# Two transformer blocks on one core: how the split fp32r operands are laid out in on-chip memory

## The chip, the cores and the metric

The kernel runs on one core of one Trainium2 chip. The metric is the device time of one execution in microseconds. Before the change it is 1729.82 us (median of 3 runs, 1728.46 to 1733.68).

## What is computed

512 tokens of width 1024 pass through two different blocks. The first adds 16 meta tokens in front (528 positions), projects, runs sliding-window attention, forgetting attention and a gated linear recurrence, merges the three, and ends with a gated feed-forward layer. The second projects again, runs a chunked mLSTM and differential attention, merges them, and ends with 32 routed experts of which each token uses two.

```python
def reference(x, ...):
    x = first_block(x, ...)   # 512 tokens and 16 meta tokens
    return second_block(x, ...)

# first_block
u = rms_norm(h, norm_mix[l]);  proj = u @ w_in[l]
merged = (g[:, :, 0] * (o_a @ w_branch[l, 0]) + g[:, :, 1] * (o_f @ w_branch[l, 1])
          + g[:, :, 2] * (o_c @ w_branch[l, 2]))
h = h + merged @ w_out[l]
gate_ff, up_ff = jnp.split(rms_norm(h, norm_ffn[l]) @ w_ffn_in[l], 2, axis=-1)
h = h + (jax.nn.silu(gate_ff) * up_ff) @ w_ffn_out[l]

# second_block
proj = (rmsnorm(x, norm1_w[l]) * (1.0 + scale1) + shift1) @ w_in[l]
merged = jax.nn.sigmoid(g_m) * (hm @ w_br_m[l]) + jax.nn.sigmoid(g_d) * (hd @ w_br_d[l])
x = x + gate1 * (merged @ w_out[l])
x = x + gate2 * hierarchical_moe(h2, ...)
```

## The kernel before

**The dense products.** Every dense weight matrix comes in slabs of 1 MB: 8 chunks of 128 rows by 256 columns (4 by 512 for the branch products, 2 by 1024 for `w_ffn_out`). SyncE loads slab `h` into `raw`, ScalarE rounds it to fp32r in `WH` (L976), VectorE writes the rest into `WL` (L1506), which has the same place as `raw`. The activations are split in the same way into a high and a low part. A group of outputs (one PSUM bank, 128 features by 512 tokens) takes three matmuls for each chunk of the contraction, in `split3`: high weight by high activation (L2365), high weight by low activation (L2366), low weight by high activation (L2367). With 8 chunks a group has 24 matmuls. In the trace's names the moving operand stands first: `psum<-AH,WH` streams AH against weights WH. Only the value projections (`vf`, `vm`, `vd`) turn this round: the activations are loaded as weights and 256 columns of WH or WL are streamed.

**The order.** The list `SLABS` of `plan_dense` sets it: `xc`, `fl`, `kf` (positions in two halves of 264 columns), `vf`, `qf`, `yc`, `qa`, `kava`, the gates and branches of the first block, `wo`, the feed-forward pair `ffg`/`ffu`, `ffo`, then the second block's projections, gates, branches, `wo2`, and last the expert loop. TensorE runs the list in order. In the two mixing stretches (MIX_FLOW, FLOW2) one piece of a dense group (12 matmuls, or a whole group of a branch) is followed by a few attention matmuls, in an order that is written out by hand.

**Where the operands lie.** Tensors stand at fixed places, in KB from a common base (`at(name, kb, shape)`). The places of the operands of `split3` (a view of AHt from column 16 starts 64 B into the row):

| tensor | place, KB | row | used by |
|---|---|---|---|
| AH (view of AHt from column 16) | 26 | 528 columns, 2112 B | all projections, `wo`, `ffg`/`ffu`, second block, `wo2` |
| AL (same view of ALt) | 42.5 | 2112 B | the same |
| WL / raw, 3 buffers of 8 KB | 59 | 1 KB or 2 KB | all |
| WH, 2 buffers of 8 KB | 83 | the same | all |
| OH | 99 + 52.8125 + 42.75 = 194.5625 | 512 columns, 2048 B | first block's branches |
| OL0, OL1, OL2 | 99, 107, 115 | 2048 B | the same |
| FH, FLo | 99, 143 | 2048 B | `ffo` |
| AHu, ALu | 146.5, 162.5 | 2048 B | `ffg` 0 and `ffu` 0 only |
| OH2, OL2 | 107, 115 | 2048 B | second block's branches |

Of the kernel before, what the change touches and what calls it, by code (L numbers as in the profile page):

```python
# [16 lines left out]
F32 = mybir.dt.float32  # L17
F32R = mybir.dt.float32r
BF16 = mybir.dt.bfloat16
I32 = mybir.dt.int32  # L20
U32 = mybir.dt.uint32
ALU = mybir.AluOpType
# [3 lines left out]
P = 128  # L26
D = 1024
KC = D // P
S = 512
M = 16  # L30
T = S + M
# [3 lines left out]
C1 = W1 // P  # L35
# [197 lines left out]
SLAB_OF = {s["name"]: s for s in SLABS}  # L233
# [136 lines left out]
def build_program(nc, a, out):  # L370

    ctx = ExitStack()
    with ctx:
# [15 lines left out]
        def at(name, kb, shape, dt=F32):  # L389
            return nc.alloc_sbuf_tensor_at(name, [P] + list(shape), dt, offset=int(base + kb * KB))[:]  # L390


        cst = at("cst", 0, [CTOT])
        pcol = at("pcol", 5.5, [2 * P])
        ones = at("ones", 6.5, [P])
        small = at("small", 7.0, [256])
        identb = at("identb", 8.0, [P], BF16)
        maskb = at("maskb", 8.25, [P], BF16)
        maskT = at("maskT", 9.5, [P])
        sinkb = at("sinkb", 8.5, [16])  # L400
        rel = at("rel", 8.5625, [8])
        fbias = at("fbias", 8.625, [4])
        mod = at("mod", 8.75, [48])
        rb = at("rb", 9.0, [36])
        stat = at("stat", 9.25, [64])
        hT = at("hT", 10, [KC, S])

        AHt = at("AH", 26, [KC, T], F32R)
        ALt = at("AL", 42.5, [KC, T], F32R)
        AH, AL = AHt[:, :, M:], ALt[:, :, M:]  # L410
        raw = at("raw", 59, [RAW, SLAB])

        WL = at("WL", 59, [RAW, SLAB], F32R)
# [16 lines left out]
        Z0 = W0 + 52.8125  # L430
        stage = at("stage", W0, [8, SKEW])
        utmp = at("utmp", Z0 + 12, [2, S])
# [6 lines left out]
        Sb = at("Sb", Z0 + 16.5, [4, 400])  # L439
        PT = at("PT", Z0 + 22.75, [2, 4 * P])  # L440
        merged = at("merged", Z0 + 26.75, [KC, S])
        OH = at("OH", Z0 + 42.75, [C1, S], F32R)
        g1a = at("g1a", Z0 + 50.75, [2, S])
        vt = at("vt", Z0 + 50.75, [T])
        g1b = at("g1b", W0 + 24, [2, S])
        g2a = at("g2a", W0 + 28, [2, S])
        g2b = at("g2b", W0 + 36.8125, [4, S])
# [182 lines left out]
        for s in SLABS:  # L630
            if s["kind"] == "W":
                n = s["h"] % RAW
                _c[n] += 16 * len(slab_dmas(s, raw[:, n, :]))
                landed[s["n"]] = (f"raw_landed{n}", _c[n])
            else:
                n = s["a"] % ARAW
# [34 lines left out]
        for n in range(0, N_PARTS, 2):  # L671
            u = parts[n]
# [285 lines left out]
        def _(act):  # L958
# [48 lines left out]
            for u in range(2 * NB):  # L1007
                t, half = u // 2, u % 2
                act.wait_ge(*when("xt_ready", u + 1))
                nc.scalar.activation(hT[:, 4 * half:4 * half + 4, P * t:P * t + P],  # L1010
                                     bank(4 + u % 2).rearrange("p (k n) -> p k n", k=4), ACT.Copy
                                     ).then_inc(S_("xt_copied"), 1)
                act.wait_ge(*when("un_ready", u + 1))
                nc.scalar.activation(AH[:, 4 * half:4 * half + 4, P * t:P * t + P],
                                     utmp[:, u % 2, :].rearrange("p (k n) -> p k n", k=4), ACT.Copy
                                     ).then_inc(S_("uh_ready"), 1)
            act.wait_ge(*when("um_ready", 1))
# [472 lines left out]
        def _(dve):  # L1490
            V = nc.vector
# [34 lines left out]
            def un_lo(u):  # L1526
                t, half = u // 2, u % 2
                dve.wait_ge(*when("uh_ready", u + 1))
                V.tensor_tensor(AL[:, 4 * half:4 * half + 4, P * t:P * t + P], utmp[:, u % 2, :].rearrange("p (k n) -> p k n", k=4),
                                AH[:, 4 * half:4 * half + 4, P * t:P * t + P].bitcast(F32), ALU.subtract  # L1530
                                ).then_inc(S_("ul_ready"), 1)

            for u in range(2 * NB):
# [820 lines left out]
        def _(pe):  # L2354
# [14 lines left out]
            def pieces(s):  # L2369
# [9 lines left out]
                    n, nk = 512, C1  # L2379
                wh = WH[:, h % HL, 0:nk * n].rearrange("p (k n) -> p k n", k=nk)  # L2380
                wl = WL[:, h % RAW, 0:nk * n].rearrange("p (k n) -> p k n", k=nk)
                rh, rl = AH, AL
                if k == "branch":
                    rh, rl = OH, OLs[MIXERS[name[1]]]
                if k == "branch2":
# [5 lines left out]
                for j, g in enumerate(s["outs"]):  # L2391
# [13 lines left out]
                    for c in range(nk):  # L2405
                        first, last = c == 0, c == nk - 1
                        if split and j == 0:
                            pe.wait_ge(*when(split, c + 1))
                        if k == "branch" and j == 0:
                            pe.wait_ge(*when("m1_ol", C1 * name[1] + c + 1))  # L2410
                        if c == nk // 2 and in_halves(g):
                            yield
                        if g[0] in ("vf", "vm", "vd"):
                            lh = AHt[:, c, 0:M] if meta else AH[:, c, P * g[2]:P * g[2] + P]
                            ll = ALt[:, c, 0:M] if meta else AL[:, c, P * g[2]:P * g[2] + P]
                            ins = split3(dst[0:M, 0:n] if meta else dst[:, 0:n], lh, ll, wh[:, c, :], wl[:, c, :], first, last)
                        else:
                            o = P if g[0] == "vt" else (g[1] * P) % n
                            lh, ll = wh[:, c, o:o + P], wl[:, c, o:o + P]
                            if len(g) == 3:  # L2420
                                ins = split3(dst[:, 0:T // 2], lh, ll, AHt[:, c, TOK[g[2]]], ALt[:, c, TOK[g[2]]], first, last)
                            else:
                                ins = split3(dst, lh, ll, rh[:, c, :], rl[:, c, :], first, last)
# [538 lines left out]
```

## Time and profile before

| | |
|---|---|
| time, median of 3 | 1729.82 us |
| span of the profiled execution | 1729.6 us |
| TensorE matmuls | 8255, busy 1601.8 us, 93% |
| weight loads (overlap the matmuls) | 1202.2 us, 70% |
| VectorE / ScalarE | 811.2 us, 47% / 544.8 us, 31% |
| DMA | 260.44 MB, mean 151 GB/s |
| mean granted TensorE clock | 0.972 |
| matmuls of `split3` with AH or AL and 512 columns | 1032 on each of three lines |

The page gives no time of the profiled execution besides its span. Matmuls are pipelined: one that is listed as 390 ns long may have the next one start 227 ns later. What a matmul costs in a run of them is therefore the distance from start to start, which is read from the timeline: the start of the last of a run less the start of the first, divided by the number of steps between them.

### The profile page before, as it was taken

To read this page: it belongs to the slowest core of one execution; us is meant where nothing else is said; L and a number is where in the kernel's file an instruction comes from. 1 tells how busy PE (TensorE), PEld (TensorE's weight loads), DVE (VectorE), ACT (ScalarE), POOL (GpSimd) and SP (SyncE) were. 2 spreads that over 40 slices of the span, in tenths; PEclk is the share of its full clock that TensorE was granted. 3 is DMA by queue.
4 is the path that set the end of the run, shared out by engine and by line. 5 is a ranking of instruction groups with operands and counts; after the bars stand their busy time and mean duration, and the time that the engine had idled before them with its cause. 6 is when DMAs were issued, how large, how long until landed. Compare 5 with 4: busy or idle time off the path is not lost.

```text
span 1729.6 us, 20154 instructions
## 1 busy us (share of the span) xinstructions
PE 1601.8 (93%) x8255; PEld 1202.2 (70%) x8255; DVE 811.2 (47%) x1399; ACT 544.8 (31%) x883; POOL 78.3 (5%) x99
## 2 busy tenths in 40 slices
PE   3999999999999999999999999999999994888785
PEld 3997777777788788888886687797678882333332
DVE  4456343454464767666223873426652715222111
ACT  5234353444433322222112433322353322111010
POOL 4000000000000000000000010000000001121111
PEclk8999999999999999999999999999999996999998
DMA  4333321222232555565223132211113617999995
GB/s 136 110 99 91 106 73 50 73 74 74 61 94 97 164 182 187 190 196 179 92 97 93 60 112 85 86 49 64 59 50 146 225 54 301 397 414 402 405 409 189
DMA packets 146800, 260.44 MB, mean 151 GB/s; under 512 B 16424, under 2 KB 121044, under 8 KB 133392
## 3 DMA queue, kind: packets, MB, share of 16 engines
q1 hardware_dynamic: 138512, 241.44, 39.6%
q0 software_dynamic: 8192, 17.67, 3.6%
q8 instruction: 67, 1.10, 0.3%
q14 instruction: 29, 0.24, 0.0%
HBM read 253.79 MB, written 15.25 MB: 156 GB/s over the span
## 4 chain that ended last, share of the span: by engine, by line
PE 84%; DVE 7%; issue 4%; ACT 2%; DMA 2%; POOL 0%; SPq 0%; POOLq 0%; DVEq 0%; ACTq 0%
PE psum L2365 20%; PE psum L2366 19%; PE psum L2367 19%; PE psum L2913 7%; PE psum L2930 3%; PE psum L2663 1%; PE psum L2652 1%; PE psum L2635 1%; PE psum L2891 1%; DMA Xg<-h_rows,tok 1%; DVE cst L1930 1%; DVE WL L1506 1%; PE psum L2562 1%; ACT Sb L1065 1%; PE psum L2582 1%
## 5 line engine op out<-in xcount | busy, mean ns | idle before, releaser
L2365 PE MATMUL psum<-AH,WH 128*128 128x512 f32 (+1 forms) x1208 | 478.8, 396 | 14.0 <-DVE AL L1552 6.3
L2366 PE MATMUL psum<-AL,WH 128*128 128x512 f32 (+1 forms) x1208 | 462.4, 383 | 0.0
L2367 PE MATMUL psum<-AH,WL 128*128 128x512 f32 (+1 forms) x1208 | 459.6, 380 | 0.0
L1506 DVE TENSOR_TENSOR WL<-raw,WH 128x2048 fp32r<-128x2048 f32 (+1 forms) x100 | 226.6, 2266 | 179.4 <-ACT WH L976 178.9
L2365 PEld LDWEIGHTS psum<-AH,WH 128*128 128x128 f32 x1208 | 230.0, 190 | 70.1 <-issue 12.3
L2367 PEld LDWEIGHTS psum<-AH,WL 128*128 128x128 f32 x1208 | 230.2, 191 | 45.1
L2366 PEld LDWEIGHTS psum<-AL,WH 128*128 128x128 f32 x1208 | 230.4, 191 | 43.6 <-issue 3.1
L976 ACT ACTIVATE WH<-raw 128x2048 fp32r<-128x2048 f32 (+1 forms) x100 | 189.0, 1890 | 137.3 <-PE psum L2367 104.2
L2913 PE MATMUL psum<-WE,XT 128*64 128x512 f32 x544 | 130.1, 633 | 13.9 <-issue 11.9
L2913 PEld LDWEIGHTS psum<-WE,XT 128*64 128x64 f32 x544 | 47.4, 146 | 94.3 <-issue 94.3
L2930 PE MATMUL psum<-WE,AT 128*64 128x512 f32 x272 | 63.9, 612 | 28.2 <-issue 26.6
L1930 DVE SCALAR_TENSOR_TENSOR cst<-araw,pcol,cst 128x256 f32<-128x256 f32 x168 | 81.6, 486 | 6.0
L1475 ACT ACTIVATE sA<-psum 128x256 f32<-128x256 f32 x17 | 6.5, 384 | 203.5 <-PE psum L2913 203.5
L2365 PE MATMUL psum<-FH,WH 128*128 128x512 f32 x176 | 68.6, 390 | 0.0
L2367 PE MATMUL psum<-FH,WL 128*128 128x512 f32 x176 | 68.5, 389 | 0.0
L2366 PE MATMUL psum<-FLo,WH 128*128 128x512 f32 x176 | 68.5, 389 | 0.0
L2365 PE MATMUL psum<-OH,WH 128*128 128x512 f32 x160 | 66.2, 414 | 0.0
L2329 DVE TENSOR_TENSOR sA<-sA,psum 128x256 f32<-128x256 f32 x17 | 7.2, 421 | 124.3 <-ACT sA L1475 124.3
L2366 PE MATMUL psum<-OL,WH 128*128 128x512 f32 x160 | 63.0, 394 | 0.0
L2367 PE MATMUL psum<-OH,WL 128*128 128x512 f32 x160 | 62.8, 393 | 0.0
L2930 PEld LDWEIGHTS psum<-WE,AT 128*64 128x64 f32 x272 | 21.9, 140 | 58.7 <-issue 58.7
L2365 PE MATMUL psum<-WH,AH 128*128 128x256 f32 (+1 forms) x208 | 59.5, 286 | 0.9 <-DVE vf L2080 0.9
(517 smaller groups left out, 2009.9 us busy)
## 6 DMA issues: line engine op xcount, KB each, us to landing
raw<-w_in SPq DMA_DIRECT2D x45, 1024.0 KB, 5.3
WE<-w_gate SPq DMA_DIRECT2D x34, 1024.0 KB, 21.9
WE<-w_up SPq DMA_DIRECT2D x34, 1024.0 KB, 24.9
WE<-w_down SPq DMA_DIRECT2D x34, 1024.0 KB, 25.1
araw<-w_ada SPq DMA_DIRECT2D x24, 1024.0 KB, 5.3
raw<-w_ffn_in SPq DMA_DIRECT2D x22, 1024.0 KB, 7.8
raw<-w_ffn_out SPq DMA_DIRECT2D x11, 1024.0 KB, 4.8
raw<-w_out SPq DMA_DIRECT2D x8, 1024.0 KB, 5.1
```

What stands on the lines that cost most here:

```text
L976: nc.scalar.activation(WH[:, fed[0] % HL, 0:w], raw[:, fed[0] % RAW, 0:w], ACT.Copy).then_inc(S_("hi_ready"), 1)
L1065: nc.scalar.activation(p, p, ACT.Exp, scale=-1.0, bias=peak, accum_out=stat[:, 20 + m % 4:21 + m % 4]).then_inc(S_("mix_exp"), 1)
L1506: V.tensor_tensor(WL[:, n, 0:w], raw[:, n, 0:w], WH[:, fed[0] % HL, 0:w].bitcast(F32), ALU.subtract).then_inc(S_("lo_ready"), 1)
L1930: ins = V.scalar_tensor_tensor(acc, w[:, c, :], col("c_2", c), acc, ALU.mult, ALU.add)
L2365: MM(dst, lh, rh, start=first, stop=False)
L2366: MM(dst, lh, rl, start=False, stop=False)
L2367: return MM(dst, ll, rh, start=False, stop=last)
L2562: MM(bank(2 + 2 * (n % 2) + m, P * (i + 1)), qkd[half, 0, h, P * i:P * i + P], qkd[half, 1, h, 0:P * (i + 1)], start=True, stop=False)
L2582: ins = MM(bank(7, P, P * i), vd[:, j, P * h:P * h + P], dPT[:, m % 2, P * j:P * j + P], start=j == 0, stop=j == i)
L2635: made = [MM(bank(2 + m % 3, parts[m]["L"]), parts[m]["q"], parts[m]["k"], start=True, stop=parts[m]["mask"] is None) for m in (n, n + 1)]
L2913: ins = MM(bank(3)[rows], XT[:, t % 2, P * k + CAP * half:P * k + CAP * half + CAP], WE[(2 * t + half) % SLOTS][:, 0:KC * 2 * DE].rearrang ...
L2930: ins = MM(bank(4 + n)[rows], AT[:, t % 2, P * j + CAP * half:P * j + CAP * half + CAP], WE[(2 * t + half) % SLOTS][:, o:o + 512], start=j ...
```

## The change

AH and AL are now two sets of views. Up to the last gate of the first block they are the views of the 528-column rows (`AHm`, `ALm`); from `wo` on they are tensors of their own with rows of 512 columns, at the same place as the wide ones. The wide tensors themselves lie at 24.5 KB and 42.5 KB, 18 KB apart, in place of 26 and 42.5. To make room the small tensors and `hT` move down by up to 1.5 KB, and `pcol` and `maskT` move to 41 and 42 KB. OH moves from 194.5625 KB to 195 KB, and `g1a` and `vt` behind it by as much. No instruction is added or taken away, no wait changes, and each matmul reads as many columns as before.

```diff
-        pcol = at("pcol", 5.5, [2 * P])
-        ones = at("ones", 6.5, [P])
-        small = at("small", 7.0, [256])
-        identb = at("identb", 8.0, [P], BF16)
-        maskb = at("maskb", 8.25, [P], BF16)
-        maskT = at("maskT", 9.5, [P])
...
-        hT = at("hT", 10, [KC, S])
-
-        AHt = at("AH", 26, [KC, T], F32R)
+        ones = at("ones", 5.5, [P])
+        small = at("small", 6.0, [256])
+        identb = at("identb", 7.0, [P], BF16)
+        maskb = at("maskb", 7.25, [P], BF16)
...
+        hT = at("hT", 8.5, [KC, S])
+
+
+        AHt = at("AH", 24.5, [KC, T], F32R)
+        pcol = at("pcol", 41, [2 * P])
+        maskT = at("maskT", 42, [P])
         ALt = at("AL", 42.5, [KC, T], F32R)
-        AH, AL = AHt[:, :, M:], ALt[:, :, M:]
+        AHm, ALm = AHt[:, :, M:], ALt[:, :, M:]
+        AH = at("AHs", 24.5, [KC, S], F32R)
+        AL = at("ALs", 42.5, [KC, S], F32R)
...
-        OH = at("OH", Z0 + 42.75, [C1, S], F32R)
-        g1a = at("g1a", Z0 + 50.75, [2, S])
-        vt = at("vt", Z0 + 50.75, [T])
+        OH = at("OH", Z0 + 43.1875, [C1, S], F32R)
+        g1a = at("g1a", Z0 + 51.1875, [2, S])
+        vt = at("vt", Z0 + 51.1875, [T])
...
-                rh, rl = AH, AL
+                rh, rl = (AHm, ALm) if h < SLAB_OF[("wo", 0)]["h"] else (AH, AL)
...
-                            lh = AHt[:, c, 0:M] if meta else AH[:, c, P * g[2]:P * g[2] + P]
-                            ll = ALt[:, c, 0:M] if meta else AL[:, c, P * g[2]:P * g[2] + P]
+                            lh = AHt[:, c, 0:M] if meta else rh[:, c, P * g[2]:P * g[2] + P]
+                            ll = ALt[:, c, 0:M] if meta else rl[:, c, P * g[2]:P * g[2] + P]
```

The writers of the first normalisation (ScalarE at L1014, VectorE at L1529) write `AHm` and `ALm` in place of `AH` and `AL`.

## Rows read from the trace of the kernel before

**Rows 1.** The page: engines' busy time, and shares of the chain that ended last.
```profile
PE 1601.8 (93%) x8255; PEld 1202.2 (70%) x8255; DVE 811.2 (47%) x1399; ACT 544.8 (31%) x883; POOL 78.3 (5%) x99
...
PE 84%; DVE 7%; issue 4%; ACT 2%; DMA 2%; POOL 0%; SPq 0%; POOLq 0%; DVEq 0%; ACTq 0%
```

**Rows 2.** Groups by line and form, engine PE: busy us, mean ns, idle before.
```profile
L2365 PE MATMUL psum<-AH,WH 128*128 128x512 f32 x1032 | 426.8, 414 | 7.7 <-DVE WL L1506 4.1 <-DVE AL L1690 3.5
...
L2365 PE MATMUL psum<-FH,WH 128*128 128x512 f32 x176 | 68.6, 390 | 0.0
...
L2365 PE MATMUL psum<-AH,WH 128*128 128x264 f32 x176 | 51.9, 295 | 6.3 <-DVE AL L1552 6.3
```

**Rows 3.** Timeline, PE: start us, length; first and last of 528 matmuls on FH, FLo.
```profile
819.18 0.48 PE L2365 MATMUL psum<-FH,WH 128*128 128x512 f32 x1
...
938.78 0.39 PE L2367 MATMUL psum<-FH,WL 128*128 128x512 f32 x1
```

**Rows 4.** Timeline, PE: second and last of 48 matmuls, one slab of `ffg`/`ffu`.
```profile
719.27 0.39 PE L2366 MATMUL psum<-AL,WH 128*128 128x512 f32 x1
...
729.93 0.39 PE L2367 MATMUL psum<-AH,WL 128*128 128x512 f32 x1
```

**Rows 5.** Timeline, PE: 96 matmuls on OH2, OL2, then 60 of `wo2`.
```profile
1339.88 0.40 PE L2365 MATMUL psum<-OH,WH 128*128 128x512 f32 x1
...
1361.43 0.39 PE L2367 MATMUL psum<-OH,WL 128*128 128x512 f32 x1
1361.65 0.40 PE L2365 MATMUL psum<-AH,WH 128*128 128x512 f32 x1
...
1375.38 0.39 PE L2367 MATMUL psum<-AH,WL 128*128 128x512 f32 x1
```

**Rows 6.** Timeline, PE: 96 matmuls on OH, OL, then 96 of `wo`.
```profile
482.96 0.40 PE L2365 MATMUL psum<-OH,WH 128*128 128x512 f32 x1
...
505.13 0.40 PE L2367 MATMUL psum<-OH,WL 128*128 128x512 f32 x1
505.36 0.40 PE L2365 MATMUL psum<-AH,WH 128*128 128x512 f32 x1
...
527.38 0.39 PE L2367 MATMUL psum<-AH,WL 128*128 128x512 f32 x1
```

**Rows 7.** Timeline, PE: second and last of 60 matmuls on AHu, ALu.
```profile
566.38 0.39 PE L2366 MATMUL psum<-ALu,WH 128*128 128x512 f32 x1
...
579.56 0.39 PE L2367 MATMUL psum<-AHu,WL 128*128 128x512 f32 x1
```

**Rows 8.** Timeline, PE: 263 matmuls with 264 columns, second to last of a run.
```profile
69.40 0.28 PE L2366 MATMUL psum<-AL,WH 128*128 128x264 f32 x1
...
101.30 0.29 PE L2367 MATMUL psum<-AH,WL 128*128 128x264 f32 x1
```

**Rows 9.** Timeline, PE, 256 columns: 24 with 16-column weights, then 192 with 128-column weights.
```profile
132.30 0.28 PE L2365 MATMUL psum<-WH,AH 128*16 128x256 f32 x1
...
134.91 0.28 PE L2367 MATMUL psum<-WH,AL 128*16 128x256 f32 x1
...
1019.15 0.28 PE L2365 MATMUL psum<-WH,AH 128*128 128x256 f32 x1
...
1041.73 0.28 PE L2367 MATMUL psum<-WH,AL 128*128 128x256 f32 x1
```

**Rows 10.** Stretches: us, busy us of PE, PEld, DVE, ACT, POOL, granted clock, DMA share, GB/s.
```profile
527.50:819.00 291.50, 287.83 (x1321) 236.52 (x1319) 189.96 (x290) 85.00 (x89) 0.00 (x0) 0.99 0.53 173
819.00:939.00 120.00, 120.00 (x531) 99.23 (x531) 31.53 (x27) 23.25 (x16) 0.00 (x0) 1.00 0.28 92
...
1320.00:1421.00 101.00, 101.00 (x516) 85.09 (x515) 43.42 (x64) 28.41 (x33) 0.00 (x0) 1.00 0.38 139
```

**Rows 11.** Waits of PE, 30 to 1430 us: who for whom, us, times, longest.
```profile
PE psum L2663 <- DVE Sb L1902: 4.9, 6, 1.0
```

**Rows 12.** The chain that ended last, in the expert loop: start us, us, what.
```profile
1666.81 3.42 issue
```

More of the change, by code:

```diff
@@ L393, in build_program @@
         cst = at("cst", 0, [CTOT])
-        pcol = at("pcol", 5.5, [2 * P])
-        ones = at("ones", 6.5, [P])
-        small = at("small", 7.0, [256])
-        identb = at("identb", 8.0, [P], BF16)
-        maskb = at("maskb", 8.25, [P], BF16)
-        maskT = at("maskT", 9.5, [P])
[L400 to L405, printed above, removed]
-        hT = at("hT", 10, [KC, S])
-        AHt = at("AH", 26, [KC, T], F32R)
+        ones = at("ones", 5.5, [P])
+        small = at("small", 6.0, [256])
+        identb = at("identb", 7.0, [P], BF16)
+        maskb = at("maskb", 7.25, [P], BF16)
+        sinkb = at("sinkb", 7.5, [16])
+        rel = at("rel", 7.5625, [8])
+        fbias = at("fbias", 7.625, [4])
+        mod = at("mod", 7.75, [48])
+        rb = at("rb", 8.0, [36])
+        stat = at("stat", 8.25, [64])
+        hT = at("hT", 8.5, [KC, S])
+        AHt = at("AH", 24.5, [KC, T], F32R)
+        pcol = at("pcol", 41, [2 * P])
+        maskT = at("maskT", 42, [P])
         ALt = at("AL", 42.5, [KC, T], F32R)
-        AH, AL = AHt[:, :, M:], ALt[:, :, M:]
+        AHm, ALm = AHt[:, :, M:], ALt[:, :, M:]
+        AH = at("AHs", 24.5, [KC, S], F32R)
+        AL = at("ALs", 42.5, [KC, S], F32R)
         raw = at("raw", 59, [RAW, SLAB])
@@ L1013, in _ @@
                 act.wait_ge(*when("un_ready", u + 1))
-                nc.scalar.activation(AH[:, 4 * half:4 * half + 4, P * t:P * t + P],
+                nc.scalar.activation(AHm[:, 4 * half:4 * half + 4, P * t:P * t + P],
                                      utmp[:, u % 2, :].rearrange("p (k n) -> p k n", k=4), ACT.Copy
@@ L1528, in un_lo @@
                 dve.wait_ge(*when("uh_ready", u + 1))
-                V.tensor_tensor(AL[:, 4 * half:4 * half + 4, P * t:P * t + P], utmp[:, u % 2, :].rearrange("p (k n) -> p k n", k=4),
-                                AH[:, 4 * half:4 * half + 4, P * t:P * t + P].bitcast(F32), ALU.subtract
+                V.tensor_tensor(ALm[:, 4 * half:4 * half + 4, P * t:P * t + P], utmp[:, u % 2, :].rearrange("p (k n) -> p k n", k=4),
+                                AHm[:, 4 * half:4 * half + 4, P * t:P * t + P].bitcast(F32), ALU.subtract
                                 ).then_inc(S_("ul_ready"), 1)
```

## The prediction, made before the changed kernel was run

> **What bounds the kernel now.** I read the shares of the page first, then the chain: TensorE is busy 93% of the span and carries 84% of the chain that ended last [rows 1]. The groups by form come next [rows 2]: the three lines of `split3` lead, and nearly all the idle time before them has two causes at the starts of stages. The table of stretches says the same of the stages: in the feed-forward pair PE is busy 287.8 of 291.5 us with VectorE at 65% and the DMA share at 0.53, and from 1320 to 1421 us PE is never idle [rows 10]. So what a dense matmul costs is paid on the path, from its start to the next one's start. Busy means don't show that cost, since matmuls overlap; the timeline does.
>
> The timeline holds a comparison of placements, all of it at the full 2.4 GHz clock, with the same 512 columns, the same weights' place and the same three lines:
> - FH and FLo, rows of 2048 B, both at an odd KB (the same place modulo 2 KB): 119.60 us for 527 steps, 226.9 ns each [rows 3].
> - AHu and ALu, rows of 2048 B, both at 0.5 KB modulo 2 KB: 13.18 us for 58 steps, 227.2 ns [rows 7].
> - OH2 and OL2, rows of 2048 B, same place: 21.55 us for 95 steps, 226.8 ns [rows 5].
> - OH and OL of the first block, rows of 2048 B, but at 0.5625 and 1 KB: 22.17 us for 95 steps, 233.4 ns [rows 6].
> - AH and AL, rows of 2112 B, 16.5 KB from each other and so 512 B apart modulo 2 KB: 10.66 us for 46 steps, 231.7 ns in the feed-forward pair [rows 4]; 22.02 for 95, 231.8 in `wo` [rows 6]; 13.73 for 59, 232.7 in `wo2` [rows 5].
>
> The three pairs in step agree within 0.4 ns, with DMA and VectorE quite different around them; the two pairs out of step cost 5 to 6.6 ns more, and right next to them: at 1361.43 us the cost changes within one step. The branch case shows that dense rows alone aren't enough. What the rows can't tell apart is whether the 2112 B row costs anything once the pair is in step, since no pair before has that.
>
> **The change part by part.** Nothing is issued more or less, so each term is a count times a difference.
>
> *1. Feed-forward pair and `wo`.* 40 groups on AH (44 less the 4 on AHu) and 8 of `wo`, 24 matmuls each: 1152. They get the layout of AHu and ALu exactly (rows of 2048 B at 24.5 and 42.5, 0.5 KB modulo 2 KB). 231.8 less 226.9 is 4.9 ns: 5.6 us.
>
> *2. Second block.* 45 groups, less `if`, which waits for its operands one chunk at a time: 44 by 24 is 1056. The difference is 5.9 ns in `wo2` beside OH2 [rows 5], 4.9 elsewhere [rows 4]; I take the middle, 5.4: 5.7 us.
>
> *3. First block's branches.* 24 groups of 12, 288 matmuls, OH now at 195 KB, the place of OL modulo 2 KB, as OH2 and OL2 lie: 6.6 ns by 288 is 1.9 us [rows 5, 6].
>
> These three make 13.2 us.
>
> *4. Projections of the first block, 512 columns.* 36 groups, 864 matmuls. Rows stay 2112 B, but AHm and ALm are now in step. Bounds: nothing (the row length or a start off a coarser boundary is what costs), or the whole 4.9 ns, 4.2 us. In the branches, being out of step cost the whole 6.6 ns with dense rows, which speaks for the upper end; the starts there were also only 64 B aligned, which speaks for the lower. Half: 2.1 us. A loss below nothing has no row for it, and is the third rival.
>
> *5. Projections with 264 columns.* 528 matmuls. 31.90 us for 262 steps is 121.8 ns [rows 8, 2]; 264/512 of 226.9 is 117.0. Bounds 0 and 2.5 us; half is 1.3 us.
>
> *6. AH as weights in the second block.* 16 value groups, 384 matmuls with 256 columns: 22.58 us for 191 steps is 118.2 ns; with only 16 columns of weights 2.61 for 23, 113.5 [rows 9], which is half of 226.9. So loading 128 columns from AH seems to cost 4.7 ns. Whether it is the place of AH that does this, no row tells: bounds 0 and 1.8 us, half 0.9. The first block's value groups keep their rows and get nothing.
>
> *7. What isn't on TensorE's path.* Of the waits of PE, one for softmax tiles of VectorE comes back 6 times, 4.9 us in all [rows 11]: there the attention chain is the bound, and dense matmuls before it that end earlier make PE wait longer. These waits are all in the first mixing stretch. I take 1.5 us off. The feed of slabs isn't near: VectorE is 65% busy in the pair [rows 10], and a slab of 48 matmuls takes some 11 us against one subtraction. The moved small tensors, `hT` and `pcol` keep their instructions and waits: nothing.
>
> *8. The expert loop.* It is partly bound by weights from memory: in the late part PE waits 3.42 us before the next 32 matmuls [rows 12]. But the first loads that this stream lacks at the start are released by the last dense group (`dense_ready`), and the others by the loop itself, so the whole stream starts earlier by what the dense part gains. Nothing is lost here.
>
> Sum: 13.2 + 2.1 + 1.3 + 0.9 - 1.5 = 16.0 us. The profiled execution's span of 1729.6 becomes 1713.6. The median of the runs is 0.2 above the span: 1713.8.
>
> **The rivals.**
>
> *A. Place doesn't matter; the difference has another cause.* The Trainium skill says so in "SBUF — State Buffer", "Who interferes with whom": TensorE has two read ports, one for the moving operand and one for weight loads, independent of each other, and never waits on anyone. The same page ("Operand start alignment") asks only for a start at a multiple of the element's size, and says that this is about legality and not speed. By that rule a shift of 64 B or 448 B would change nothing, which is the time before, 1729.8. As a mechanism of this kernel: the dearer stretches would be so because of what VectorE, ScalarE or DMA do meanwhile. Against it: `ffo` has a DMA share of 0.28, the pair 0.53 [rows 10], but the branches of the second block, at 226.8, lie in a stretch with 0.38, between two runs on AH at 231 to 233. The change between rates comes with the operand, at 1361.43 us [rows 5]. Traces bear the rule out only for FH, AHu and OH2. 1729.8 within 5; chance 0.08.
>
> *B. In step isn't what counts, only part is won.* Rows of 2048 B win, but the pair's position does something else in AH's region: terms 1 and 2 alone, at half rate, and nothing for 4 to 6, is 5.7 + 1.9 - 1.5 = 6.1 us: 1723.7. For it: each row of 2112 B starts 64 B further on than the one before, and no row prices that by itself. Chance 0.05.
>
> *C. Being in step is what collides, for rows of 2112 B or in this region: slower.* The place would be every matmul of `split3` on AHm/ALm and, if the region matters, on AH/AL. Price: the 6.6 ns of the branch case [rows 6] on 864, and half of it on 528 with 264 columns: 5.7 + 1.7 = 7.4 us lost in the first block. With terms 1 to 3 won, that is still a gain of 5.8. It decides against the change once AH/AL in the new place lose too: at 4.9 ns lost in place of won on 2208 matmuls, 10.8 + 7.4 - 1.9 = 16.3 us, 1746.1. Against it: AHu and ALu have this very place modulo 2 KB with the same WH and WL [rows 7]. Chance 0.02.
>
> *D. The wait takes the place of the gain.* All of the second block's and first block's mixing stretches bound by their attention chains: terms 2 to 5 mostly gone, 5.6 + 2 us remain, 1722.2. Against it: PE's waits there are 4.9 us in all [rows 11]. Chance 0.05.
>
> **How the numbers follow.** My forecast has 0.80: 1713.8. Its own span: with terms 4 to 6 whole (4.2 + 2.5 + 1.8) and nothing off, 21.7 us gained, 1708.1; with 4 to 6 at nothing and 3 us off for waits, 10.2 gained, 1719.6. The runs before scatter by 1.4 below and 3.9 above their median, so I widen by some 1.3: 1706.8 to 1721. B and D stay outside, with A and C: that leaves out 0.20. A measurement of this kernel tells apart about 0.3%, 5.2 us. Faster by more than that: forecast, B, D and a little of nothing else, 0.90; within it, A and what of B falls short, 0.08; slower 0.02.
>
> **What would show it right or wrong.** In the trace after, `wo`, `ffu` and `wo2` must step at 226.8 to 227.5 ns, and the first block's branches too. The gates of the first block decide term 4: 232 (nothing) or 227 (whole). The 264-column runs: 121.8 or 117. The value groups of the second block: 118.2 or 113.5; those of the first block unchanged. The stretch from the start of `ffg` to the end of `ffo` should shrink by about 5 us, the one from there to the end of `wo2` by about 6 to 7, and the expert loop not at all. I am wrong if matmuls on AH stay at 231.8, which is A, or if they step at 227 and PE's idle time grows by the same, which is D; and the clock may hide a few us if half-rate windows fall differently.

## The result, and the profile after

The changed kernel takes 1722.79 us (median of 6 runs, 1722.32 to 1725.15). The kernel before, with three runs more beside it, has a median of 1732.74 us (1728.46 to 1733.68). The ratio is 0.995, with a 95% interval of 0.9936 to 0.9965: faster by half a percent, some 10 us, but outside the range I gave, which ended at 1721.0.

The span of the profiled execution goes from 1729.6 to 1720.6 us, 9.0 less against a forecast of 16.0. Its own time was 1722.53 us, so the span lies 1.9 us under the time, as in every run here that has both (1.75 to 1.93); I had taken 0.2.

The page of the changed kernel: span, engines, shares of the chain, and the largest group of its matmuls (busy us, mean ns of one, idle before).

```profile
span 1720.6 us, 20154 instructions
...
PE 1592.7 (93%) x8255; PEld 1203.9 (70%) x8255; DVE 811.1 (47%) x1399; ACT 544.9 (32%) x883; POOL 78.0 (5%) x99
...
PE 82%; DVE 8%; issue 4%; ACT 3%; DMA 2%; POOL 0%; SPq 0%; POOLq 0%; DVEq 0%; ACTq 0%
...
L2368 PE MATMUL psum<-AHs,WH 128*128 128x512 f32 x744 | 306.8, 412 | 7.7 <-DVE WL L1509 5.2
```

Beside [rows 1], PE's busy time falls by 9.1 us with the same 8255 matmuls, and the chain's PE share by two points. AHs is the dense view; its 744 triples are the ones from `wo` on.

Timeline of PE after: 96 matmuls of the last branch, then 96 of `wo`; the answer to [rows 6].

```profile
480.62 0.40 PE L2368 MATMUL psum<-OH,WH 128*128 128x512 f32 x1
...
502.16 0.39 PE L2370 MATMUL psum<-OH,WL 128*128 128x512 f32 x1
502.39 0.39 PE L2368 MATMUL psum<-AHs,WH 128*128 128x512 f32 x1
...
523.92 0.39 PE L2370 MATMUL psum<-AHs,WL 128*128 128x512 f32 x1
```

21.54 us for 95 steps is 226.7 ns in the branch, where it was 233.4; 21.53 for 95 is 226.6 in `wo`, where it was 231.8. Rows at the new places run at the rate of FH. So far the reasoning holds. In the first block's projections the cost hasn't changed. After: 263 matmuls of 264 columns, then 144 of 512 columns on the wide rows:

```profile
67.50 0.28 PE L2369 MATMUL psum<-AL,WH 128*128 128x264 f32 x1
...
99.40 0.29 PE L2370 MATMUL psum<-AH,WL 128*128 128x264 f32 x1
...
148.63 0.48 PE L2368 MATMUL psum<-AH,WH 128*128 128x512 f32 x1
...
181.87 0.39 PE L2370 MATMUL psum<-AH,WL 128*128 128x512 f32 x1
```

And the kernel before in the second of these runs:

```profile
150.41 0.48 PE L2365 MATMUL psum<-AH,WH 128*128 128x512 f32 x1
...
183.65 0.39 PE L2367 MATMUL psum<-AH,WL 128*128 128x512 f32 x1
```

31.90 us for 262 steps, as in [rows 8], and 33.24 us for 143 steps, 232.4 ns, in both kernels: not a hundredth of a microsecond came from having the pair in step. The `vm` groups of the second block, AH as weights (compare [rows 9], 118.2 ns):

```profile
1013.46 0.28 PE L2368 MATMUL psum<-WH,AHs 128*128 128x256 f32 x1
...
1036.37 0.28 PE L2370 MATMUL psum<-WH,ALs 128*128 128x256 f32 x1
```

22.91 us for 191 steps, 119.9 ns: each has become 1.7 ns dearer.

The next rows are a slab of the feed-forward pair after, right behind the column sums of `w_ada` (matmuls of one column), and its last matmul:

```profile
598.76 0.49 PE L2368 MATMUL psum<-AHs,WH 128*128 128x512 f32 x1
599.09 0.40 PE L2369 MATMUL psum<-ALs,WH 128*128 128x512 f32 x1
599.32 0.40 PE L2370 MATMUL psum<-AHs,WL 128*128 128x512 f32 x1
599.55 0.40 PE L2368 MATMUL psum<-AHs,WH 128*128 128x512 f32 x1
599.79 0.39 PE L2369 MATMUL psum<-ALs,WH 128*128 128x512 f32 x1
600.01 0.39 PE L2370 MATMUL psum<-AHs,WL 128*128 128x512 f32 x1
600.25 0.40 PE L2368 MATMUL psum<-AHs,WH 128*128 128x512 f32 x1
...
601.17 0.39 PE L2369 MATMUL psum<-ALs,WH 128*128 128x512 f32 x1
601.40 0.39 PE L2370 MATMUL psum<-AHs,WL 128*128 128x512 f32 x1
...
609.56 0.40 PE L2370 MATMUL psum<-AHs,WL 128*128 128x512 f32 x1
```

Steps of 330, 230, 230, 240, 220, 240 ns, and only at 601.17 us do they become even; to the nanosecond the trace has 324, 235, 233, 236, 224, 231, 236, 228, 233, 231, and then 226 and 227 up to the end of the slab. The first ten steps behind an interruption cost what they cost before. Not every slab needs ten: of the 18 whole slabs from here on, 11 need nine or ten, and 7 are even after three (318, 232, 231, 227). The slab of [rows 4] took 231.7 ns a step; this one takes 10.47 us for 46 steps, 227.6.

Where the 9.0 us came from, by the starts of the same matmul in both traces (both have 8255 in the same order; durations in us):

| stretch, up to the first matmul of the next one | before | after | difference |
|---|---|---|---|
| start to `qf` (150.41 before) | 150.41 | 148.63 | -1.78 |
| `qf` to last branch | 332.55 | 331.98 | -0.57 |
| last branch | 22.40 | 21.77 | -0.63 |
| `wo` up to `ffu` 0, second half (566.07) | 60.71 | 59.66 | -1.05 |
| to the slab at 601.62 | 35.55 | 36.71 | +1.16 |
| feed-forward pair from 601.62 | 217.56 | 214.30 | -3.26 |
| `ffo`, norms, start of the second block | 172.64 | 171.50 | -1.14 |
| first projections of the second block | 27.33 | 28.90 | +1.57 |
| `vm` and the second mixing stretch | 301.19 | 299.87 | -1.32 |
| undisturbed gates | 19.54 | 19.16 | -0.38 |
| second block's last branches | 21.77 | 21.76 | -0.01 |
| `wo2` | 46.94 | 46.54 | -0.40 |
| router and expert loop, to the span's end | 321.05 | 319.86 | -1.19 |

Step by step the layout's part can be told from the rest. From `qf` to the router, over all steps from one matmul's start to the next that touch no time at half clock in either trace, the changed kernel is 8.9 us shorter; the steps that do touch such time are 2.9 us longer in sum. By kind of matmul, in us:

| steps | number | difference |
|---|---|---|
| AH, AL in `wo` and the pair (term 1) | 1114 | -5.02 |
| AH, AL in the second block (term 2) | 949 | -3.67 |
| OH, OL in the first block (term 3) | 272 | -1.03 |
| wide rows, 512 columns (term 4) | 765 | -0.14 |
| wide rows, 264 columns behind `qf`'s start (term 5) | 92 | 0.00 |
| AH, AL as weights in the second block (term 6) | 361 | +0.56 |
| all others, waits included | 2628 | +0.37 |

Some of the gain went into longer waits of PE for VectorE. In the pair PE waits behind every fourth slab for the column sums of `w_ada`; the view of waits for the pair, before and then after:

```profile
PE psum L2485 <- DVE cst L1930: 0.8, 4, 0.2
```

```profile
PE psum L2488 <- DVE cst L1933: 1.2, 4, 0.3
```

That is 0.46 us by the steps. In `wo2` the wait for the low part of a slab costs two steps 400 and 335 ns where they were 229 and 248, 0.26 us more, which is in the row of term 2.

The two losses in the table of stretches are mostly the clock's. The stretch up to 601.62 in the table of stretches (us, busy us of PE, PEld, DVE, ACT, POOL, granted clock, DMA share, GB/s), first before, then after, then in the first kernel of the experiments (AL 512 B further), which has the same work there:

```profile
566.07:601.62 35.55, 32.63 (x139) 26.39 (x138) 30.00 (x44) 15.71 (x19) 0.00 (x0) 0.95 0.53 171
```

```profile
562.05:598.76 36.71, 33.52 (x139) 27.20 (x138) 30.00 (x44) 15.71 (x19) 0.00 (x0) 0.91 0.54 172
```

```profile
563.53:597.41 33.88, 30.70 (x140) 25.14 (x138) 29.71 (x43) 15.71 (x19) 0.00 (x0) 1.00 0.50 161
```

At a granted clock of 1.00, full 2.4 GHz throughout, it takes 33.88 us; at 0.95 it is 35.55 and at 0.91 36.71, a longer part of the stretch at 1.2 GHz each time. In each of the three PE waits in this stretch for VectorE's low part of a slab. The step there is 3.31 us before, 3.58 after and 3.57 in the third kernel. So 0.27 us of the 1.16 is this wait. The same wait goes with full clock in one and with 0.91 in the other. The second loss lies where the second block begins; the same table, before and then after:

```profile
949.00:1019.00 70.00, 64.58 (x264) 48.20 (x265) 60.14 (x89) 29.34 (x37) 4.77 (x9) 0.93 0.21 65
```

```profile
943.00:1013.40 70.40, 65.49 (x264) 49.93 (x265) 61.12 (x91) 29.19 (x36) 4.78 (x9) 0.88 0.23 70
```

PE waits here for the norm's operands, and the granted clock is 0.93 before and 0.88 after. One step, before the slab at 999.63 us, grows from 1.49 to 2.24 us in a wait for the slab's low part, which is 0.75 of the 1.57.

### The profile page after: what moved, and what is told of

It reads as the page before. It is cut to its first block, busy times and chain, and to the rows that moved or that the text cites. A ratio compares the mean times of both kernels' runs of the same rounds, so it can differ in the third digit from the quotient of the medians.

```text
span 1720.6 us, 20154 instructions
## 1 busy us (share of the span) xinstructions
PE 1592.7 (93%) x8255; PEld 1203.9 (70%) x8255; DVE 811.1 (47%) x1399; ACT 544.9 (32%) x883; POOL 78.0 (5%) x99
## 4 chain that ended last, share of the span: by engine, by line
PE 82%; DVE 8%; issue 4%; ACT 3%; DMA 2%; POOL 0%; SPq 0%; POOLq 0%; DVEq 0%; ACTq 0%
PE psum L2368 20%; PE psum L2369 19%; PE psum L2370 19%; PE psum L2916 7%; PE psum L2933 3%; PE psum L2666 1%; PE psum L2655 1%; PE psum L2638 1%; PE psum L2894 1%; DMA Xg<-h_rows,tok 1%; DVE cst L1933 1%; DVE WL L1509 1%; PE psum L2565 1%; ACT Sb L1068 1%; DVE qkm L1720 1%
## 5 line engine op out<-in xcount | busy, mean ns | idle before, releaser
L2368 PE MATMUL psum<-AHs,WH 128*128 128x512 f32 x744 | 306.8, 412 | 7.7 <-DVE WL L1509 5.2
L1509 DVE TENSOR_TENSOR WL<-raw,WH 128x2048 fp32r<-128x2048 f32 (+1 forms) x100 | 226.6, 2267 | 179.3 <-ACT WH L979 178.8
L2370 PE MATMUL psum<-AHs,WL 128*128 128x512 f32 x744 | 293.1, 394 | 0.0
L2369 PE MATMUL psum<-ALs,WH 128*128 128x512 f32 x744 | 293.0, 394 | 0.0
L2368 PE MATMUL psum<-AH,WH 128*128 128x512 f32 (+1 forms) x464 | 170.2, 367 | 6.3 <-DVE AL L1555 6.3
L2368 PEld LDWEIGHTS psum<-AHs,WH 128*128 128x128 f32 x744 | 141.6, 190 | 43.5 <-DVE WL L1509 6.1
L2369 PE MATMUL psum<-AL,WH 128*128 128x512 f32 (+1 forms) x464 | 165.0, 356 | 0.0
L2370 PE MATMUL psum<-AH,WL 128*128 128x512 f32 (+1 forms) x464 | 164.2, 354 | 0.0
L2369 PEld LDWEIGHTS psum<-ALs,WH 128*128 128x128 f32 x744 | 142.0, 191 | 30.8 <-issue 3.1
L2370 PEld LDWEIGHTS psum<-AH,WL 128*128 128x128 f32 x464 | 88.4, 191 | 12.4
L2369 PEld LDWEIGHTS psum<-AL,WH 128*128 128x128 f32 x464 | 88.4, 191 | 10.4
```

What stands on the lines that cost most here:

```text
L1509: V.tensor_tensor(WL[:, n, 0:w], raw[:, n, 0:w], WH[:, fed[0] % HL, 0:w].bitcast(F32), ALU.subtract).then_inc(S_("lo_ready"), 1)
L2368: MM(dst, lh, rh, start=first, stop=False)
L2369: MM(dst, lh, rl, start=False, stop=False)
L2370: return MM(dst, ll, rh, start=False, stop=last)
```

## The experiments

Two theories stood at the start. S: the two operands must be at the same place modulo 2 KB. L: each row must start on a coarse boundary, and the pair's relation is of no account. The trace of the changed kernel already speaks for L, since the wide rows are in step now and cost the same. All these kernels leave everything else as it is, the order of the instructions too.

**AL 512 B further, out of step.** Each stage from `wo` on gets its own pair of tensors, and its writers and readers use it (these lines are left out here); `PLACES` has the bytes by which AH and AL are moved up in `wo`, the pair (`ff`), the second block (`two`) and `wo2` (`wt`).

```diff
-        AH = at("AHs", 24.5, [KC, S], F32R)
-        AL = at("ALs", 42.5, [KC, S], F32R)
+
+        PLACES = {'wo': (0, 512), 'ff': (0, 512), 'two': (0, 512), 'wt': (0, 512)}
+        AHx = {k: at("AH" + k, 24.5 + h / KB, [KC, S], F32R) for k, (h, l) in PLACES.items()}
+        ALx = {k: at("AL" + k, 42.5 + l / KB, [KC, S], F32R) for k, (h, l) in PLACES.items()}
...
```

> Changed kernel, with AL (rows of 2048 B, from `wo` on) moved up by 512 B, so that AH and AL are 512 B apart modulo 2 KB, as in the kernel before; all rows still start on multiples of 512 B. Theory S (the pair must be in step): the runs of `wo` go from 226.7 ns a matmul back to 231 to 233, those of the feed-forward pair too, and the time rises by some 7 us towards that of the kernel before. Theory L (each row must start on a coarse boundary, the pair's relation is of no account): `wo` stays at 226.7 ns and the time stays within 2 us of the changed kernel's, near 1722.8.

1725.01 us, median of 7; 0.9958 of the kernel before, interval 0.9943 to 0.9972. That is 2.2 us above the changed kernel's 1722.79, which was not timed beside it, a little more than the 2 expected, and the two intervals overlap; the span of the profile is 1720.5 us, as the changed kernel's. The first 96 matmuls of `wo`:

```profile
503.87 0.39 PE L2370 MATMUL psum<-AHwo,WH 128*128 128x512 f32 x1
...
525.40 0.39 PE L2372 MATMUL psum<-AHwo,WL 128*128 128x512 f32 x1
```

21.53 us for 95 steps: 226.6 ns. S has fallen. The 18 KB, and the same place modulo 2 KB, bring nothing by themselves.

**Both moved up by 32 to 256 B, in step.** Against the kernel above only `PLACES` differs; here and in the later ones the line with the minus is that of the kernel named.

```diff
-        PLACES = {'wo': (0, 512), 'ff': (0, 512), 'two': (0, 512), 'wt': (0, 512)}
+        PLACES = {'wo': (256, 256), 'ff': (64, 64), 'two': (128, 128), 'wt': (32, 32)}
```

> Changed kernel with AH and AL in step (18 KB apart) but both moved up: by 256 B in `wo`, 64 B in the feed-forward pair, 128 B in the second block, 32 B in `wo2`. Theory S: every stage stays as in the changed kernel: `wo` 226.7 ns, an undisturbed slab's later matmuls 226.7, the gates of the second block 226.7. Theory L: some of them return to about 232 ns, surely the 32 and 64 B ones, and the coarsest that does names the boundary. The value groups of the second block (AH as weights, 120.0 ns in the changed kernel, 118.2 before) tell whether the weights' start counts: at 128 B they come back to about 118 by L, stay at 120 by S.

The first 96 matmuls of `wo`, up by 256 B:

```profile
503.93 0.39 PE L2370 MATMUL psum<-AHwo,WH 128*128 128x512 f32 x1
...
525.47 0.39 PE L2372 MATMUL psum<-AHwo,WL 128*128 128x512 f32 x1
```

21.54 us for 95: 226.7 ns. With 64 B the last 24 steps of a slab of the pair have a mean of 228.9 ns, with 128 B those of the second block's undisturbed gates 232.1, and with 32 B the first 47 steps of `wo2` 233.4, where the changed kernel has 226.7 in all of them. The value groups, up by 128 B, cost 118.6 ns in place of 119.9. So 0, 256 and, for AL, 512 B reach 226.7, and 32, 64 and 128 B don't; 192 B was not tried.

The kernel before says the same. In its `wo` the steps repeat every 12 matmuls, which are four chunks: 228, 234, 233, 226, 236, 227, 233, 233, 233, 233, 232, 232 ns, 231.7 on the mean. After four chunks rows of 2112 B have drifted by 256 B. The one chunk in four that does begin on a multiple of 256 B isn't at 226.7 either (226, 236, 228), so a step's length isn't set by its own matmul's row alone.

**Only one of the two moved.** Against the last kernel:

```diff
-        PLACES = {'wo': (256, 256), 'ff': (64, 64), 'two': (128, 128), 'wt': (32, 32)}
+        PLACES = {'wo': (0, 64), 'ff': (0, 256), 'two': (64, 0), 'wt': (0, 128)}
```

> Changed kernel with only one of the two moved up: AL by 64 B in `wo`, AL by 256 B in the feed-forward pair, AH by 64 B in the second block, AL by 128 B in `wo2`. Theory S: all out of step, so all at 231 to 233 ns. Theory L: in `wo` only matmuls that stream AL or follow one are dearer, so a mean between 226.7 and 232, about 229; the 256 B stage as in-step 256 B; the second block (AH, two of three matmuls) about 230.

The first 96 matmuls of `wo`, with AL up by 64 B:

```profile
506.14 0.39 PE L2370 MATMUL psum<-AHwo,WH 128*128 128x512 f32 x1
...
528.17 0.39 PE L2372 MATMUL psum<-AHwo,WL 128*128 128x512 f32 x1
```

22.03 us for 95 steps, 231.9 ns: dearer than both moved by 64 B (228.9), and dearer than my 229. AL alone up by 256 B leaves the pair at 226.7. AH alone up by 64 B puts the undisturbed gates at 233.3. In `wo2`, with AL up by 128 B, the first 47 steps repeat as 227, 234, 226 (229.0 on the mean): only the one from the AL matmul to the next is dearer. Behind the interruptions that follow, the same operands repeat as 236, 234, 230 in some runs, 233.3 on the mean. So off the boundary one place has more than one steady rate, and which of them comes depends on how the run starts. All in all 256 B is what counts for each operand, but off it the pair's relation has a say too: 64 B for both costs 2.2 ns, for one of them 5 to 7. The value groups have AH and AL as weights: with AH alone up by 64 B they cost 118.5 ns.

**The branch operand alone, on the kernel before.**

```diff
-        OH = at("OH", Z0 + 42.75, [C1, S], F32R)
-        g1a = at("g1a", Z0 + 50.75, [2, S])
-        vt = at("vt", Z0 + 50.75, [T])
+        OH = at("OH", Z0 + 43.1875, [C1, S], F32R)
+        g1a = at("g1a", Z0 + 51.1875, [2, S])
+        vt = at("vt", Z0 + 51.1875, [T])
```

> Kernel before with the second part of the change alone: OH at 195 KB, g1a and vt behind it. The last branch (96 matmuls, undisturbed) goes from 233.4 to 226.7 ns by both theories. The branches inside the mixing stretch gain less, because each is followed by other matmuls: in all the first block's end at the last branch moves by about 1 us and the whole time by 1 us or less, against 1.9 in my sum.

The last branch takes 21.77 us as in the changed kernel (22.40 before), and the stretch from `qf` to it 332.04 (332.55 before): 1.14 us in all. The one run's time, 1734.64, lies inside the scatter of the kernel before (1727.98 to 1735.62 beside it); what 1.1 us does to the whole it can't tell. Term 3 alone is thus 1.14 us in place of 1.9.

**Dense rows in the first block too.** The products are not the reference's here, which the expectation says; this prices the stage only, and the whole time (1724.22 us) is not compared.

```diff
-                rh, rl = (AHm, ALm) if h < SLAB_OF[("wo", 0)]["h"] else (AH, AL)
+                first_h, first_l = (x.rearrange("p k t -> p (k t)")[:, 0:KC * S].rearrange("p (k n) -> p k n", k=KC) for x in (AHt, ALt))
+                rh, rl = (first_h, first_l) if h < SLAB_OF[("wo", 0)]["h"] else (AH, AL)
```

> Changed kernel in which the first block's projections without meta columns and its value groups read the wide tensors' memory as if its rows had 512 columns: 864 matmuls of 512 columns and 192 value matmuls then start each row on a multiple of 512 B. What they multiply is not what the reference multiplies, so the activations are wrong and the routing may differ; only stages before the expert loop are compared. Theory L with the cut theory (a matmul gains only some ten matmuls after the last interruption): the undisturbed run that starts near 150 us goes from 232.4 to about 227 ns a matmul, 0.8 us, the run of 60 before the last branch too; in the mixing stretch pieces of 12 gain little. In all the last branch starts 1.2 to 2 us earlier, against the 4.2 us that 4.9 ns on each of 864 would bring.

The 144 matmuls that ran at 232.4 ns:

```profile
152.31 0.47 PE L2368 MATMUL psum<-AH,WH 128*128 128x512 f32 x1
...
184.93 0.39 PE L2370 MATMUL psum<-AH,WL 128*128 128x512 f32 x1
```

32.62 us for 143: 228.1. From the first of them to the last branch the stretch takes 330.16 us, 1.82 less than in the changed kernel (331.98). Inside my 1.2 to 2, against the 4.2 of "every matmul gains 4.9". In the mixing stretch the gain goes on at 0.07 to 0.19 us for each 250 matmuls, of which some 50 to 150 are dense ones on AH or AL and would bring 0.2 to 0.7 at 4.9 ns each. Term 4 had a real price, then, but needs dense rows.

**`wo` cut into pieces of 12.** The same lines in both kernels:

```diff
                         if c == nk // 2 and in_halves(g):
                             yield
+                        if k == "wo" and c % 4 == 0:
+                            for _ in range(4):
+                                MM(bank(6, 1), ones, ones[:, 0:1], start=True, stop=True)
```

> Changed kernel with four dummy matmuls of one column (ones by ones, into an unused bank) before every twelfth matmul of `wo`: 16 interruptions. Cut theory: between two interruptions the first 4 to 10 steps are dearer than 226.7 ns, so a piece of 12 costs 60 to 140 ns more than undisturbed beside the dummies themselves, and the gain of the rows of 2048 B over the kernel before with the same cuts falls from 1.0 us over `wo` (192 matmuls) to 0.1 to 0.6 us. Rival (every matmul gains alike, and the missing part of the gain went into half-rate clock windows alone): the gain over the kernel before with cuts stays at 1.0 us.

> Kernel before with the same dummy matmuls in `wo`. Reference for the run above. Both theories: its pieces of 12 keep their 232 ns a step and lengthen only by the dummies and by the first step after them.

The start of `wo`, kernel before with cuts (each fp32 dummy stands as two matmuls in the trace, so eight):

```profile
505.26 0.95 PE L2415 MATMUL psum<-ones 128*128 128x1 f32 x8
506.07 0.48 PE L2365 MATMUL psum<-AH,WH 128*128 128x512 f32 x1
```

Changed kernel with cuts:

```profile
503.04 0.95 PE L2418 MATMUL psum<-ones 128*128 128x1 f32 x8
503.85 0.49 PE L2368 MATMUL psum<-AHs,WH 128*128 128x512 f32 x1
```

The first twelve of the sixteen pieces, 144 matmuls, in the table of stretches: the kernel before with cuts, then the changed one.

```profile
505.26:552.88 47.62, 47.62 (x274) 41.25 (x272) 18.32 (x21) 13.05 (x16) 0.00 (x0) 1.00 0.21 68
```

```profile
503.04:550.55 47.51, 47.51 (x273) 41.23 (x272) 18.32 (x21) 13.22 (x17) 0.00 (x0) 1.00 0.21 68
```

At a granted clock of 1.00 the gain of the layout over these 144 matmuls is 0.1 us. Without cuts the same 144 took 36.87 us before (505.36 to 542.23) and 36.13 after: 0.74. In the thirteenth piece of both kernels the granted clock is 0.5 for a while (from 553.63 us and from 551.58), so the whole of `wo` tells less; it takes 63.72 us against 63.60, where it took 47.87 (505.36 to 553.23) and 46.88 (502.39 to 549.27) without cuts. The whole programs, timed once each, take 1744.43 us and 1739.27.

In a piece of the kernel before the steps are 321, 232, 232, 231, 232, 228, 234, 233, 233, 226, 236; of the changed one 324, 235, 233, 236, 224, 231, 236, 228, 233, 231, 226. So in the changed kernel a piece is over by the time its steps reach 226.7. One of its pieces, the ninth, is an exception: 318 and then 227, 227, 226 from the second step on. The cut theory holds for the others, and the rival (every matmul gains alike) doesn't.

**Places again, in other stages.** Against the kernel with both moved by 32 to 256 B:

```diff
-        PLACES = {'wo': (256, 256), 'ff': (64, 64), 'two': (128, 128), 'wt': (32, 32)}
+        PLACES = {'wo': (128, 128), 'ff': (128, 128), 'two': (64, 64), 'wt': (256, 0)}
```

> Changed kernel with AH and AL from `wo` on in other places: both up by 128 B in `wo` and in the feed-forward pair, both up by 64 B in the second block, AH up by 256 B and AL not in `wo2`. If a multiple of 256 B is the boundary whatever the pair's relation: `wo2` 226.7 ns; 128 B gives 232 in `wo` as it did in the second block, 64 B gives 229 in the second block as it did in the pair. If the stage mattered and not the start, the numbers stay with the stages: 232 in the second block and 226.7 in `wo`.

`wo`, both up by 128 B, and the value groups of the second block, up by 64 B:

```profile
502.77 0.40 PE L2370 MATMUL psum<-AHwo,WH 128*128 128x512 f32 x1
...
524.94 0.39 PE L2372 MATMUL psum<-AHwo,WL 128*128 128x512 f32 x1
...
1017.02 0.28 PE L2370 MATMUL psum<-WH,AHtwo 128*128 128x256 f32 x1
...
1038.69 0.28 PE L2372 MATMUL psum<-WH,ALtwo 128*128 128x256 f32 x1
```

22.17 us for 95 steps, 233.4 ns in `wo`, and the pair 232.0 to 233.3 over the last 24 steps of a slab: 128 B is dear in every stage. The gates at 64 B have 228.9 as the pair had. AH up by 256 B with AL in place leaves the first 47 steps of `wo2` at 226 and 227. The numbers go with the start and not with the stage, up to 1.3 ns for 128 B. What I had not foreseen: the value groups at 64 B take 21.67 us for 191 steps, 113.5 ns. That is the rate of the 16-column weights in [rows 9]. So the place of AH and AL does decide what these groups cost, but the boundary that is good for them as moving operands is the worst of those tried for them as weights: 119.9 with both at 0 B, 118.6 with both at 128 B, 118.5 with AH alone at 64 B, 118.2 in the kernel before, 113.5 with both at 64 B.

The three kernels that only moved operands within stages ran once each as a whole: 1724.42 us (32 to 256 B), 1729.26 (only one moved) and 1724.54 (this one). Runs of one kernel scatter by some us, so only the stages are read from them.

**The second block alone at 64 B, timed beside the changed kernel.** Against the kernel with both moved by 32 to 256 B:

```diff
-        PLACES = {'wo': (256, 256), 'ff': (64, 64), 'two': (128, 128), 'wt': (32, 32)}
+        PLACES = {'wo': (0, 0), 'ff': (0, 0), 'two': (64, 64), 'wt': (0, 0)}
```

The changed kernel itself was timed once more beside it, with no edit:

> The changed kernel itself, timed beside the next one: 1721 to 1725 us.

> Changed kernel with AH and AL of the second block alone both up by 64 B; `wo`, the feed-forward pair and `wo2` as in the change. The value groups (192 `vm` matmuls undisturbed, 192 `vd` in the mixing stretch) go from 120.0 to 113.5 and about 116 ns, 1.3 and 0.8 us; the undisturbed gates and first projections of the second block lose 2.2 ns a matmul, some 0.4 us; pieces in the mixing stretch cost the same. From the first `vm` matmul to the first gate of the undisturbed run 1.0 to 1.3 us less, over the whole 1 us less than the changed kernel: at the edge of what five rounds tell. If only the pair's relation or only the moving rows' start counted, the value groups would stay at 120.0 ns and the whole would be 0.5 us slower.

The first and the last of the `vm` matmuls of the kernel with this edit:

```profile
1011.01 0.28 PE L2370 MATMUL psum<-WH,AHtwo 128*128 128x256 f32 x1
...
1032.67 0.28 PE L2372 MATMUL psum<-WH,ALtwo 128*128 128x256 f32 x1
```

The `vm` groups take 21.66 us where they took 22.91, so 1.25 us are won there, and the undisturbed gates lose 0.17 (19.33 against 19.16). The whole doesn't show it: 1722.68 us (median of 6, 1720.51 to 1726.84; ratio to before 0.9951, 0.9933 to 0.9969) against 1721.28 for the changed kernel on the same chip (1717.70 to 1725.97; 0.9940, 0.9920 to 0.9960), inside the 1721 to 1725 expected for it. The intervals overlap almost wholly. In the profiles the stretch from `vm` to the undisturbed gates is even longer, 301.87 us against 299.89 in the changed kernel, but at less granted clock. The kernel of "Places again, in other stages" has the same places in this block (64 B for both) and the changed kernel's granted clock, 0.99. The table of stretches for it, and then for the kernel with this edit:

```profile
1017.02:1315.65 298.63, 297.35 (x1717) 240.04 (x1716) 151.87 (x229) 105.88 (x186) 2.14 (x4) 0.99 0.24 77
```

```profile
1011.01:1312.88 301.87, 300.58 (x1718) 242.70 (x1716) 151.85 (x229) 105.81 (x186) 2.13 (x4) 0.98 0.24 76
```

298.63 against 299.89 at the same granted clock of 0.99: 1.26 us less, as expected (1.0 to 1.3). The stage gains, then, but the whole program is not measurably faster than the changed kernel.

## Why the prediction was wrong, step by step

**What bounds the kernel, and that place sets the rate: right.** Rival A, that place has no effect, is out. The Trainium skill's "SBUF — State Buffer", "Who interferes with whom", says that TensorE has two independent read ports and never waits on anyone. That section is about engines that get in each other's way; that place costs nothing, as rival A has it, was my conclusion from it and isn't stated there. Here a shift of one operand by 64 B, with every other instruction the same, moved `wo` from 226.6 to 231.9 ns a matmul, so for this kernel the measurement decides against the conclusion. What the runs don't show is the mechanism, whether the reads of weights and moving rows meet, or something else; it stays open.

**The reading of the pairs: wrong, and the source of terms 4 and 5.** I saw pairs in step at 227 ns and pairs out of step at 232 to 233 and took the step for the cause. Each pair at 227 also had rows that begin on multiples of 256 B, and each of the others rows that don't. The row of OH and OL, on which I leaned, fits both: OH began at 194.5625 KB, 64 B off. With AL moved by 512 B the two readings part, and the boundary is it. Terms 4 and 5, 2.1 and 1.3 us forecast, brought 0.1: the wide rows of 2112 B drift by 64 B with each chunk, in step or not. I had put 0 as their lower bound, so the range had this.

**Terms 1 to 3: right in sign and mechanism, sized too large.** 13.2 us were forecast and 9.7 came, by the table of steps: 5.0 in place of 5.6 for the pair and `wo`, 3.7 in place of 5.7 for the second block, 1.0 in place of 1.9 for the branches. The step that failed is "a count times a difference". The difference holds for matmuls well inside a run: in the pair the steps from the twelfth on fell from 231.7 to 226.7 ns. Behind an interruption less is won or nothing: the third to the eleventh step fell by 3.1 ns in the pair (232.5 to 229.4) and by 3.3 in the second mixing stretch (232.3 to 229.0), where 553 of the 625 steps come before the twelfth, since most runs are 12 matmuls long. `wo` with and without cuts shows it alone: 0.1 us in place of 0.74. The rows for it were in front of me: [rows 3] and [rows 7] start with the first or second matmul of a run, and I averaged over 527 and 58 steps. Read one by one, the steps behind the first matmul of [rows 3] are 324, 235, 233, 235, 224, 231, 237, 227, 234 and 230 ns, and 226 to 228 from there on.

**Term 6: wrong in sign.** I had 0.9 us gained, with no loss in its bounds. AH and AL as weights on a multiple of 256 B cost 119.9 ns for 118.2: 0.33 us lost over 191 steps of `vm`, and 0.56 over the 361 steps of `vm` and `vd` at full clock. The lower bound should have reached below nothing, since no row had both operands on the boundary with 128 columns of weights.

**Term 7: a wait in another place.** I took 1.5 us off for the waits for softmax tiles in the first mixing stretch. That wait is 4.9 us before and after, and in the whole stretch from `qf` to the last branch, which holds it, there were only 0.57 us for it to take. The waits that did grow are others, all for VectorE: for its column sums in the pair (0.46 us), which I had not looked at, and for the low part of a slab, which I had called not near, in `wo2` (0.26) and before the slab at 601.62 (0.27). That these 1.0 us are near my 1.5 is luck.

**Rivals B and D.** Both have about the measured time, 1723.7 and 1722.2, and neither is what happened. B is the nearer one: nothing for terms 4 to 6 came true, but terms 1 and 2 brought 8.7 us, not the half of 11.3. D would give the time for the wrong reason: the run with cuts has no attention in it and loses the gain all the same.

**Term 8: right.** The expert loop and the router take 319.86 us after 321.05; nothing of the gain was lost there. The 1.19 between them can't be called a gain either: the kernel before with cuts in `wo`, which has nothing of the change, has 319.77, and the profiles of the changed kernel with other places 318.98 to 320.49.

**The clock.** I wrote that it may hide a few microseconds, and gave it no term. The steps that touch time at half clock cost 2.9 us more after than before, waits in them included. It isn't tied to the layout: the kernel with the second block alone at 64 B has the very layout and work of the changed kernel up to the slab at 601.62, and took 33.89 us for that stretch in place of 36.71. The kernel with AL moved by 512 B checks the sum: from `qf` to the router it has the same mean granted clock as the kernel before, 0.992 (the changed kernel 0.988), and takes 1249.95 us there against 1258.18, 8.2 less.

**The numbers.** The layout's own gain is thus 8.2 to 8.9 us, in place of 16.0. Of the 7.1 that are missing, 3.5 are in terms 1 to 3, 3.3 in terms 4 and 5 and 1.5 in term 6; term 7 was taken too large and gives some of it back. The span's 9.0 are the 8.9, less the 2.9 at half clock, and 1.78 at the start and 1.19 at the end. The 1.78 is scatter: the first matmul of `qf` starts at 148.63 us in the changed kernel, at 150.41 in the kernel before, and anywhere from 148.95 to 152.32 in the six profiles of the experiments with the same work up to there (150.05, 150.16, 152.32, 148.95, 149.13, 149.76). And the anchor was off: I set the time 0.2 us above the span, and it is 1.9 above. The median of three runs that I started from, 1729.82, was 2.9 under that of six, 1732.74. With the span's forecast of 1713.6 and the right distance the forecast would have been 1715.5, and the range would have ended at 1722.7, a tenth of a microsecond short of the 1722.79. My range had 10.2 us of gain at its small end, less 1.4 for scatter. What was missing in it is the case that the gain per matmul doesn't hold in short runs, and a loss in term 6.

## What to carry to other kernels

Try every row of a moving fp32r operand on a multiple of 256 B: here that gave 226.7 ns for 512 columns, against 229 to 233 off it. Padding that makes rows drift (here 16 extra columns, 64 B) takes three rows of four off the boundary, and the fourth isn't at 226.7 either. Where the same operand also serves as weights, measure that too, since its best place was another one here. Price such a gain in full only for the matmuls that lie more than ten behind an interruption, and at anything from nothing to two thirds for those before. And before one reading of a comparison of rows carries the sum, list what else the cheaper rows have in common, and let the range hold that reading too.

## What the runs showed of the hardware that I had not expected

- The start modulo 256 B sets the rate, at a grain of 64 B or less: steady steps of 226.7 ns at 0 and 256 B, 228.9 at 64 B for both operands, 231.9 and 233.3 at 64 B for one, 232.0 to 233.4 at 128 B for both, 229.0 or 233.3 at 128 B for AL alone, 233.4 at 32 B for both.
- After an interruption by one-column matmuls or by a wait a run mostly needs three to ten matmuls to reach 226.7 ns. The same patterns come back to within some 2 ns (324, 235, 233, 236, 224 or 318, 232, 231, 227); what picks one of them was not tested.
- For AH and AL as weights (128 columns, 256 columns streamed) the order is the other way: 119.9 ns on the boundary, 113.5 with both at 64 B.
